# The opening of a one-core two-block transformer kernel: tokens, constants and the first weights in pieces

## The reference

```python
def rmsnorm(x, g):
    y = x32 * lax.rsqrt(jnp.mean(x32 * x32, axis=-1, keepdims=True) + EPS)
    return (y * g.astype(jnp.float32)).astype(x.dtype)
...
u = h @ w_pw1 + b_pw1                      # h = rmsnorm(x, norm_mix[0])
a, gate = jnp.split(u, 2, axis=-1)
u = a * jax.nn.sigmoid(gate)
u = depthwise_causal_conv(u, w_dw) + b_dw  # width 31
u = jax.nn.silu(layernorm(u, ln_g, ln_b))
x = x + u @ w_pw2 + b_pw2
```

## Time and profile before

| | us |
|---|---|
| median of 3 runs | 1296.5 |
| lowest, highest | 1293.46, 1297.28 |
| the profiled execution's own time | 1294.27 |
| its span, first to last instruction | 1292.9 |
| granted TensorE clock, mean | 0.979 |

### The profile page before, as it was taken

How to read it: one execution, slowest core, us unless ns; L and a number is a source line. 1 busy time by engine, 2 the same in 40 slices (tenths; PEclk the granted TensorE clock), 3 DMA queues, 4 the chain that set the end, 5 groups by cost and what they waited for, 6 DMA issues and landing times.

```text
span 1292.9 us, 24807 instructions
## 1 busy us (share of the span) xinstructions
PE 1211.4 (94%) x9924; PEld 1147.9 (89%) x9924; DVE 926.4 (72%) x1753; ACT 660.2 (51%) x1144; POOL 72.6 (6%) x82
## 2 busy tenths in 40 slices
PE   5998999999998999999988789999999879999999
PEld 5877999999987999999977668999989767999999
DVE  5637698878686888879796658888875555776652
ACT  6327554444446544446555656444444766544441
POOL 1001000001000100003000101000010112000000
PEclk9999999999999999999998989999999989999999
DMA  8852698778753687788533326887875423555561
GB/s 281 239 153 83 204 305 263 253 257 279 246 176 132 212 265 255 244 276 270 197 111 100 110 87 193 270 255 253 270 242 184 135 91 105 183 185 180 181 194 66
DMA packets 81126, 258.10 MB, mean 200 GB/s; under 512 B 8872, under 2 KB 22004, under 8 KB 81012
## 3 DMA queue, kind: packets, MB, share of 16 engines
q1 hardware_dynamic: 75252, 250.69, 59.3%
q10 hardware_dynamic: 5760, 5.83, 1.9%
HBM read 253.82 MB, written 2.67 MB: 198 GB/s over the span
## 4 chain that ended last, share of the span: by engine, by line
PE 74%; DVE 14%; ACT 6%; issue 4%; POOL 1%; DMA 1%; SPq 0%; DVEq 0%; ACTq 0%; POOLq 0%
PE ps L519 66%; DVE wlo L1232 4%; PE ps L570 2%; DVE HL L1238 1%; DVE X L1238 1%; DVE aacc L1238 1%; ACT HH L845 1%; ACT oS L845 1%; ACT eS L845 1%; PE ps L626 1%; PE ps L618 1%; ACT tmp L845 1%; DVE tmp L1546 1%; PE ps L617 1%; PE ps L622 1%
## 5 line engine op out<-in xcount | busy, mean ns | idle before, releaser
L519 PE MATMUL ps<-HH,whi 128*128 128x256 f32 (+1 forms) x2152 | 624.4, 290 | 24.9 <-DVE wlo L1232 11.9
L519 PE MATMUL ps<-HH,wlo 128*128 128x256 f32 (+1 forms) x2152 | 613.9, 285 | 0.0
L519 PE MATMUL ps<-HL,whi 128*128 128x256 f32 (+1 forms) x2152 | 613.3, 285 | 0.0
L845 ACT ACTIVATE whi<-raw 128x1024 fp32r<-128x1024 f32 x363 | 382.5, 1057 | 346.0 <-PE ps L519 337.3
L1232 DVE TENSOR_TENSOR wlo<-raw,whi 128x1024 fp32r<-128x1024 f32 x363 | 441.7, 1221 | 46.1 <-ACT whi L845 45.5
L519 PEld LDWEIGHTS ps<-HH,whi 128*128 128x128 f32 x2152 | 414.2, 192 | 43.0 <-issue 29.7
L519 PEld LDWEIGHTS ps<-HL,whi 128*128 128x128 f32 x2152 | 414.1, 192 | 0.4
L519 PEld LDWEIGHTS ps<-HH,wlo 128*128 128x128 f32 x2152 | 413.6, 192 | 0.0
L519 PE MATMUL ps<-GH,whi 128*128 128x256 f32 x704 | 198.2, 282 | 0.6 <-DVE bcol L1428 0.5
L519 PE MATMUL ps<-GH,wlo 128*128 128x256 f32 x704 | 197.5, 281 | 0.0
L519 PE MATMUL ps<-GL,whi 128*128 128x256 f32 x704 | 197.5, 281 | 0.0
(11 more groups left out here) (207 smaller groups left out, 939.2 us busy)
## 6 DMA issues: line engine op xcount, KB each, us to landing
raw<-wall SPq DMA_DIRECT2D x363, 512.0 KB, 4.3
araw<-ada SPq DMA_DIRECT2D x96, 512.0 KB, 4.7
UR<-uscr ACTq DMA_DIRECT2D x32, 142.0 KB, 4.3
oBB<-kbias SPq DMA_DIRECT2D x16, 192.0 KB, 2.6
aTB<-scratch SPq DMA_DIRECT2D x12, 128.0 KB
uscr<-U ACTq DMA_DIRECT2D x8, 143.5 KB, 3.7
X<-x_in SPq DMA_DIRECT2D x2, 512.0 KB, 5.7
out<-X SPq DMA_DIRECT2D x8, 128.0 KB, 2.8
```

The source lines that it names most:

```text
L519: ins = pe.e.matmul(o, l, r, start=(kt == p.order[0] and i == 0), stop=(kt == p.order[-1] and i == 2))
L845: ac.then_inc(ac.e.activation(o, i, func, **kw), sem)
```

## The change: the opening in pieces

X is loaded in three parts (kt 0 and 1, 2 and 3, 4 to 7), each followed by a unit; `vec` is cut at the column where `wdw` begins: its first 56 columns are loaded behind the first part of X, the rest behind unit 2. Unit 0 is split in two pieces of four blocks with signals of their own. `warm()` is called before anything else on ACT, and no longer begins with `settle()`, which the later calls get ahead of them. ACT and DVE split units 0 to 3 between the parts of HH and HL, and three, two and three squares stand behind units 1, 2 and 3. `total(0)` is issued on PE ahead of tile 0's last kt. The memsets of U move ahead of DVE's wait for `vec`. Waits for the second part of `vec` are added where it is used.

```diff
+VEC_FIRST = VCOL["wdw"]
+X_PARTS = ((0, 2), (2, 4), (4, 8))
+FIRST_BLOCKS = 4
...
                     ready(kt)
-                    pe.wait_ge(S.hi, u + 1)
-                    pe.wait_ge(S.lo, u + 1)
+                    if u == 0 and c < FIRST_BLOCKS:
+                        pe.wait_ge(S.hi0, 1)
+                        pe.wait_ge(S.lo0, 1)
+                    else:
+                        pe.wait_ge(S.hi, u + 1)
+                        pe.wait_ge(S.lo, u + 1)
...
                 def after(nt):
-                    if nt == 0:
-                        total(0)
...
-                product("pw1", HH[NORM_SET[0]], HL[NORM_SET[0]], T, norm_ready(0), after)
+                product("pw1", HH[NORM_SET[0]], HL[NORM_SET[0]], T, norm_ready(0), after,
+                        lambda kt: total(0) if kt == KD - 1 else None)
... ACT
+                    if v == 0:
+                        f = FIRST_BLOCKS * P
+                        act(whi[0][:, 0:f], raw[0][:, 0:f], ACT.Copy, S.hi0)
+                        act(whi[0][:, f:], raw[0][:, f:], ACT.Copy, S.hi)
+                        continue
...
-                    ac.wait_ge(S.x1 if nt >= 4 else S.x0, 16)
+                    ac.wait_ge(S.xs[min(nt // 2, len(X_PARTS) - 1)], 16)
...
             def warm():
-                ac.settle()
                 ac.wait_ge(S.eps, 2)
                 ac.e.activation(sc[:, 7:8], epsb[:, 0:1], ACT.Sqrt)
...
             def convolution():
+                warm()
                 ac.wait_ge(S.vec, 16)
...
                 def taps(j):
                     ac.wait_ge(S.cvt, j + 1)
+                    ac.wait_ge(S.vecb, 16)
...
                 for kt in range(KD):
                     norm_high(0, kt)
-                    if kt in (1, 3, 5):
+                    if kt % 2:
                         highs(kt // 2)
-                for kt in range(KD):
-                    square(0, kt)
+                    for m in {3: (0, 1, 2), 5: (3, 4), 7: (5, 6, 7)}.get(kt, ()):
+                        square(0, m)
... DVE
+                    if v == 0:
+                        f = FIRST_BLOCKS * P
+                        dv.wait_ge(S.hi0, 1)
+                        tt(wlo[0][:, 0:f], raw[0][:, 0:f], whi[0][:, 0:f].bitcast(F32), ALU.subtract, S.lo0)
+                        dv.wait_ge(S.hi, 1)
+                        tt(wlo[0][:, f:], raw[0][:, f:], whi[0][:, f:].bitcast(F32), ALU.subtract, S.lo)
+                        continue
...
+                dv.then_inc(dv.e.memset(U[:, :, 0:30], 0.0), S.uz)
+                dv.then_inc(dv.e.memset(U[:, :, 30 + T:31 + T], 0.0), S.uz)
                 dv.wait_ge(S.vec, 16)
                 for kt in range(KD):
                     norm_low(0, kt)
-                    if kt in (3, 5):
-                        lows(kt // 2 - 1)
-                dv.then_inc(dv.e.memset(U[:, :, 0:30], 0.0), S.uz)
-                dv.then_inc(dv.e.memset(U[:, :, 30 + T:31 + T], 0.0), S.uz)
+                    if kt % 2:
+                        lows(kt // 2)
... SP
-            load(vec[:, :], vec_in, S.vec)
-            load(X[:, 0:4, :], x_in[:, 0:4, :], S.x0)
-            load_unit()
-            load(X[:, 4:8, :], x_in[:, 4:8, :], S.x1)
-            load_unit()
+            for i, (a, b) in enumerate(X_PARTS):
+                load(X[:, a:b, :], x_in[:, a:b, :], S.xs[i])
+                if i == 0:
+                    load(vec[:, 0:VEC_FIRST], vec_in[:, 0:VEC_FIRST], S.vec)
+                load_unit()
+            load(vec[:, VEC_FIRST:], vec_in[:, VEC_FIRST:], S.vecb)
```

More of the change, by code:

```diff
@@ L329, in __init__ @@
     def __init__(self, new):
-        self.vec, self.x0, self.x1, self.k128 = new("vec"), new("x0"), new("x1"), new("k128")
+        self.vec, self.vecb, self.k128 = new("vec"), new("vecb"), new("k128")
+        self.xs = [new(f"xs{i}") for i in range(len(X_PARTS))]
         self.row, self.kdist, self.wq, self.koh = new("row"), new("kdist"), new("wq"), new("koh")
@@ L342, in __init__ @@
         self.hi, self.lo, self.mm, self.ev = new("hi"), new("lo"), new("mm"), new("ev")
+        self.hi0, self.lo0 = new("hi0"), new("lo0")
         self.hh, self.hl = new("hh"), new("hl")
@@ L934, in residual @@
                         if nt == 0:
+                            ac.settle()
                             warm()
@@ L1382, in convolution @@
                 inverse(1)
+                dv.wait_ge(S.vecb, 16)
                 for kt in range(KD + 2):
```

## The result

The changed kernel takes 1290.95 us (median of 20 runs, 1288.15 to 1296.44), the kernel before 1295.38 (20 runs, 1291.79 to 1298.67). The ratio is 0.9966, with a 95% interval of 0.9954 to 0.9977: 4.4 us faster, between 3.0 and 6.0. The profiled execution took 1290.6 us, its span is 1289.3 us, to compare with 1294.27 and 1292.9.

What follows compares the result with a forecast made beforehand. TensorE was taken to bound the kernel (74% of the span), so an earlier opening ends it earlier: first matmul -4.3 us, second wait about 0, 1296.5-4.3=1292.2 us; range 1289.3 to 1295.0.

Steps and rivals of the forecast that it cites:

- The sum: Whole opening: first matmul 4.3 us earlier, second wait about unchanged; together 4.3 us faster, 1292.2 us.
- rival 2: Opening's loads: short rows of X and vec slow the stream, second wait 2.4 us; gain 3.1, time 1293.4; chance 0.22.
- First term: Start of PE's work: first matmul at 7.6 us against 11.89, 4.3 us earlier.
- Table first: Start of ACT: table load over by about 2.5 us, 1.3 us off the front; the load before the root falls away.
- X, vec and unit 0 in pieces: Opening's loads and first split: HH at 3.9 us, unit 0 landed at 6.2, first matmul at 7.6.
- Does PE run through: PE between first matmul and second wait: units 1 to 3 ready with 1.7 to 2.2 us slack, arrival at 22.5.
- Rival 4: PE's opening: a late unit makes PE idle and the low clock last; slower, 1306.0 us; chance 0.05.
- The second wait: PE's wait for the norm's root behind unit 8, landing at 22.2 us: 1.3 us long, PE goes on at 23.8.
- the landing: Unit 8's delay after the stream passed its last byte: taken as 0.6 us, bounds 0.4 to 1.1.
- low part of unit 3: DVE's split of unit 3, ready at about 16.5 us, when unit 8's load may be issued.

Runs made afterwards that it cites:

- the loads of before: Changed kernel with vec loaded whole ahead of X and X in two halves, without the waits for vec's second part; ratio 0.9965 to the kernel before.
- the old order: Changed kernel with ACT's earlier order: all squares behind HH 7 and unit 3 split behind the squares; ratio 0.9992 to the kernel before.

## Why the prediction was right

*The sum* was 4.3 us and 4.4 were measured. That the two agree so well is in part luck: in the three profiles of the changed kernel PE goes on 3.6 to 3.9 us earlier than before, not 4.3, and in two of them a low stretch takes back 1.5 of it. The gain measured at this mark lies between the forecast's 4.3 and the 3.1 of rival 2, whose second wait of 2.4 us came in two of the three. The sum was written down as "First term -4.3 (first matmul); second wait 1.3 for 1.4, about 0". The runs show that this way of adding up names the wrong cause. With the first matmul 1.6 us later (the loads of before) the opening ends at the same time; with the earliest first matmul (the old order, 7.50) it ends 2.4 us later. What the change does to the root's chain is the gain, and the first matmul only has to be early enough.

*Table first*: the load was over before 2.3 us, and none stood before the root. Right, and what counts is the load at the root: the one at the front costs 0.6 us at the first matmul and nothing behind it.

*X, vec and unit 0 in pieces*: HH was expected at 3.9 and started at 4.66, when the short piece of vec landed (4.7, the upper bound of the forecast). Unit 0 landed at 6.2, as forecast, and hid it. First matmul 7.72 for 7.6. Rival 2, that short rows slow the stream, is in part true of the first 6 us (172 GB/s for 197, 0.4 us), but the kernel with the loads of before, which moved 185 GB/s there, reached the same 24.54. Unit 7 landed 0.7 us earlier in it, so the pieces may have slowed the stream; PE did not feel it. The late piece of vec (28 KB, 3.5 us in flight, against 3.7 for 256 KB of X) fits the rule of the Trainium skill (*DMA: Bandwidth & Descriptors*, section Specifications) that rows below 512 bytes don't reach the full rate, but it also queued behind X, and no run separates the two.

*Does PE run through*: yes; 22, 27 and 22 matmuls at the low pace in the changed kernel's three profiles and no gap. PE reached the wait at 21.9 to 22.5, forecast 22.5; the shorter low pace is what made it 0.4 to 0.6 earlier in two of them. Rival 4 in its own form (idling before unit 1) did not come.

*The second wait* was the mis-sized term: 1.3 forecast, 2.42, 1.90 and 2.37 measured. Unit 8 landed at 22.95 and 22.83 in the first two profiles, not 22.2. The stream itself was as forecast: adding up its stretches as before, it had passed 6.94 MB at 21.5 to 21.7 us, where 21.1 and 0.5 for the short rows make 21.6. What was too small is the landing behind it, 0.6 us "as nothing is queued behind", for which 1.2 to 1.3 came. Unit 9 was queued behind, issued at 20.28 and 20.02, and may have shared the stream; no run holds it back. The forecast's low part of unit 3 at 16.5 ended at 18.03; the stream was full all that time, so this probably cost little, but no run takes it away. And the step left something out: rival 4 rested on "a gap of 1.4 us doesn't" lower the clock. Behind the longer wait the low clock came in two of three executions and cost 1.5 us: from going on to the first taps they took 14.28 us, the third 12.78.

*What stays open.* The clock decides part of each execution's time, and one profile can't be set against a median. At the squares' sums the changed kernel is 1.6 to 3.7 us ahead of the one profile of before, while the medians differ by 4.4 (3.0 to 6.0), and the two later timings by 0.9971 and 0.9975. These agree if the lower end of the one and the upper end of the other are taken. The kernel before may meet the low stretch itself in some executions, as a kernel with a wait of 1.34 us did; I have one profile of it and can't say.

## What to carry to other kernels

Find the last thing that the end of an opening waits for and follow its queue back; an earlier start of the bound engine is worth only what that chain also gains. Here a root that needed nothing of unit 8 stood behind it in ScalarE's order: moving three lines took the wait away in both profiles, and that kernel was the faster both times (1287.67 beside 1291.57 us, clear of noise, then 1288.43 beside 1290.95, with intervals that overlap). Here squares that wait for GpSimd stood in the queue of the engine that splits the weights; it pays to spread them among the splits, because a load is issued only when its slot has been split. That gave 2.4 us of 3.7. And count what is issued behind the load that you wait for, too: the forecast took it as nothing, and the landing was the term that came out too small.

## What the runs showed of the hardware

**The low clock behind a wait.** Over the openings of the fourteen profiles, the low pace came back behind the root's waits of 2.37, 2.42, 2.77 and 3.18 us each time, behind those of 1.34 to 1.90 us in two of five (1.34 and 1.70 yes; 1.35, 1.38 and 1.90 no), and behind the five of 0.61 us and less never. The one of 1.34 us is no clean case, as PE had stood 2.44 us shortly before it. The three long waits for something else, 2.10 and 3.31 us for UR and 2.44 us for unit 3, were followed by it too. It began between 0 and 2 us after PE had gone on: behind the wait for UR of 2.10 us with the first matmul (49.02); in the first profile of the changed kernel PE went on at 24.53 and slowed at 26.3. Later in that same profile PE stood 2.77 us until 665.81 and 2.35 us until 962.39, and the granted clock stayed at 1.00 for the next 5 us. The page *TensorE: Matmul & The Clock Gate* of the Trainium skill (Part 1) says that idling brings the half rate back; the runs agree that it can, and show that the length of the wait alone doesn't decide it.

**DVE beside POOL's additions.** Two HL instructions in a row on DVE took 0.88 us in the kernel before, where POOL was still idle, and nearly twice that in the changed kernel, where its additions now run at the same time. The timeline of DVE, first before, then the second profile of the changed kernel:

```profile
11.66 0.88 DVE L1238 SCALAR_TENSOR_TENSOR HL<-X,vec,HH 128x256 fp32r<-128x256 f32 x2
```

```profile
11.51 1.66 DVE L1255 SCALAR_TENSOR_TENSOR HL<-X,vec,HH 128x256 fp32r<-128x256 f32 x2
...
14.23 1.85 DVE L1255 SCALAR_TENSOR_TENSOR HL<-X,vec,HH 128x256 fp32r<-128x256 f32 x2
```

The run with the old order bears it out. There the additions start at 13.75; the three pairs of HL ahead of that take 0.88 us as before, and the fourth, which meets them, takes longer:

```profile
13.43 1.35 DVE L1255 SCALAR_TENSOR_TENSOR HL<-X,vec,HH 128x256 fp32r<-128x256 f32 x2
```

The HL instruction and the addition each read two tiles of SBUF. The page *SBUF — State Buffer* of the Trainium skill (section "SBUF: two separate sides") says that such a DVE instruction and one of GpSimd lock each other out; the additions of 0.74 us each fit the 0.8 to 1.0 us that each pair lost. With the pair ahead of it 1.0 us longer and unit 3's low part itself 1.76 us instead of 1.22, this makes up the 1.5 us by which that part was later than forecast (18.03 for 16.5). No run takes the additions away.
